# Differential attention heads: the probabilities become the stationary operand of the product with the values

## The reference

```python
s = jnp.einsum('bqhtd,bkhtd->bhtqk', qb, k).astype(jnp.float32) + bias[None, :, None]
pr = jax.nn.softmax(s, axis=-1)
attn = pr[:, :, 0] - lam * pr[:, :, 1]
...
o = rmsnorm(o, subln) * (1.0 - lam_init)
o = o.reshape(b, l, ATTN_V_DIM) * jax.nn.silu(z)
return o @ w_out
```

## Time and profile before

| | |
|---|---|
| median of 3 runs | 807.06 us (806.58 to 814.43) |
| the profiled execution | 812.39 us, of which the span of the trace is 810.4 us |
| PE matmul busy | 765.7 us, 94% of the span |
| DVE, ACT, POOL busy | 506.4, 402.6, 451.3 us |

### The profile page before, as it was taken

How to read it: one execution, slowest core, us unless ns; L and a number is a source line. 1 busy time by engine, 2 the same in 40 slices (tenths; PEclk the granted TensorE clock), 3 DMA queues, 4 the chain that set the end, 5 groups by cost and what they waited for, 6 DMA issues and landing times.

```text
span 810.4 us, 11587 instructions
## 1 busy us (share of the span) xinstructions
PE 765.7 (94%) x3856; PEld 616.9 (76%) x3856; DVE 506.4 (62%) x880; ACT 402.6 (50%) x806; POOL 451.3 (56%) x258
## 2 busy tenths in 40 slices
PE   4999999999999999998999999899999999998788
PEld 3677888888878787887878887667777777776576
DVE  4674957585858677785921131676867768677732
ACT  6446483829273655657332253355555454654410
POOL 5348595848484857665754427563653745536101
PEclk9999999999999999999999999999999999999999
DMA  9265464553626364543523214322313222220002
GB/s 255 78 196 127 159 151 162 124 189 95 190 82 160 125 155 154 155 158 104 210 78 107 82 52 143 112 74 66 88 53 101 76 78 74 67 85 27 0 1 104
DMA packets 100196, 91.10 MB, mean 112 GB/s; under 512 B 5456, under 2 KB 87728, under 8 KB 97080
## 3 DMA queue, kind: packets, MB, share of 16 engines
q1 hardware_dynamic: 95760, 66.99, 28.2%
q10 hardware_dynamic: 4264, 23.50, 9.3%
q0 software_dynamic: 128, 0.05, 0.0%
HBM read 88.13 MB, written 2.39 MB: 112 GB/s over the span
## 4 chain that ended last, share of the span: by engine, by line
PE 54%; DVE 20%; issue 11%; ACT 7%; POOL 7%; DMA 1%; DVEq 1%; ACTq 0%; SPq 0%; POOLq 0%
PE bank L1351 45%; DVE c_acc L996 6%; POOL w_lo L486 3%; POOL stat L477 2%; ACT ex L836 2%; PE bank L1454 2%; DVE sbias L1218 2%; PE bank L1428 1%; PE bank L1440 1%; DVE tmp L1038 1%; DVE ex L1229 1%; ACT qkvz L901 1%; ACT w_hi L621 1%; DVE stat L1222 1%; PE bank L1402 1%
## 5 line engine op out<-in xcount | busy, mean ns | idle before, releaser
L486 POOL TENSOR_TENSOR w_lo<-w_raw,w_hi 128x1024 fp32r<-128x1024 f32 x104 | 257.4, 2477 | 224.1 <-ACT w_hi L621 224.0
L1351 PE MATMUL bank<-hn_hi,w_hi 128*128 128x512 f32 (+1 forms) x392 | 157.9, 403 | 8.0 <-DVE BT L1011 5.0
L1351 PE MATMUL bank<-hn_hi,w_lo 128*128 128x512 f32 (+1 forms) x392 | 153.8, 392 | 0.0
L1351 PE MATMUL bank<-hn_lo,w_hi 128*128 128x512 f32 (+1 forms) x392 | 153.5, 392 | 0.0
L621 ACT CAST w_hi<-w_raw 128x1024 fp32r<-128x1024 f32 x104 | 108.7, 1047 | 71.5 <-PE bank L1351 68.5
L1351 PE MATMUL bank<-w_hi,hn_hi 128*128 128x512 f32 x320 | 131.0, 409 | 4.8 <-DVE hn_lo L1102 2.5
L1351 PE MATMUL bank<-w_lo,hn_hi 128*128 128x512 f32 x320 | 125.9, 393 | 0.0
L1351 PE MATMUL bank<-w_hi,hn_lo 128*128 128x512 f32 x320 | 125.9, 393 | 0.0
L996 DVE SCALAR_TENSOR_TENSOR c_acc<-bank,par,c_acc 128x510 f32<-128x510 f32 (+1 forms) x128 | 95.9, 749 | 24.0 <-ACT c_acc L665 14.6
L836 ACT ACTIVATE ex<-sbias,stat 128x512 f32<-128x512 f32 x64 | 45.7, 716 | 120.5 <-DVE stat L1222 120.5
L1351 PEld LDWEIGHTS bank<-hn_hi,w_hi 128*128 128x128 f32 (+1 forms) x392 | 73.5, 188 | 26.7 <-issue 9.9
(11 more groups left out here) (191 smaller groups left out, 1237.0 us busy)
## 6 DMA issues: line engine op xcount, KB each, us to landing
w_raw<-in_ssd_w_in SPq DMA_DIRECT2D x48, 512.0 KB, 4.0
w_raw<-in_attn_w_in SPq DMA_DIRECT2D x64, 256.0 KB, 3.1
rows<-acs_rows ACTq DMA_DIRECT2D x14, 1024.0 KB, 5.9
edec<-exp_rows ACTq DMA_DIRECT2D x16, 512.0 KB, 6.2
w_raw<-in_ssd_w_out SPq DMA_DIRECT2D x16, 512.0 KB, 3.5
w_raw<-in_attn_w_out SPq DMA_DIRECT2D x16, 256.0 KB, 3.1
wbias<-bias_rows SPq DMA_DIRECT2D x8, 448.0 KB, 4.1
rows<-in_x SPq DMA_DIRECT2D x4, 512.0 KB, 5.2
```

The lines of the kernel that those rows point to most:

```text
L486: nc.gpsimd.tensor_tensor(w_lo[:, s, :], w_raw[:, s, :], f32(w_hi[:, s, :]), ALU.subtract)\
L1351: ins = T.matmul(dst, a[i], b[j], start=first and n == 0, stop=last and n == 2)
```

## The change

`values` computes `o` directly instead of its transpose. The stationary operand is now a 128 x 128 block of `aT_hi` or `aT_lo` (128 keys, 128 queries), the moving operand is the 128 x 128 chunk of `v_hi` or `v_lo`. For each of four blocks of queries the four chunks of keys are summed: 4 x 4 x 3 = 48 matmuls of 128 columns in place of 12 of 512. The copy of bank 7 (L851) and the first four transposes (L1590) with their two semaphores are gone; ACT squares bank 7 in stage 0, where the copy stood.

```diff
-        o_copied, o_back = sem("o_copied"), sem("o_back")
...
                     if has(3):
                         act.wait_ge(pv_done, it - 2)
                         after(act, og_done, it - 3)
-                        nc.scalar.copy(o_chan[:, :], bank[7][:, :]).then_inc(o_copied, 1)
+                        nc.scalar.activation(o_flat, bank[7][:, :], ACT.Square).then_inc(o_sqd, 1)
...
-                    if has(3):
-                        act.wait_ge(o_back, it - 2)
-                        nc.scalar.activation(o_chan[:, :], bank[7][:, :], ACT.Square).then_inc(o_sqd, 1)
...
-                for c in range(NC):
-                    ins = product(bank[7][:, :], (v_hi[:, par_, c, :], v_lo[:, par_, c, :]),
-                                  (aT_hi[:, c, :], aT_lo[:, c, :]), c == 0, c == NC - 1)
+                for q in range(NC):
+                    rows_ = slice(q * P, (q + 1) * P)
+                    for c in range(NC):
+                        ins = product(bank[7][:, rows_], (aT_hi[:, c, rows_], aT_lo[:, c, rows_]),
+                                      (v_hi[:, par_, c, :], v_lo[:, par_, c, :]), c == 0, c == NC - 1)
                 ins.then_inc(pv_done, 1)
...
-                if s == 1 and has(3):
-
-                    pe.wait_ge(o_copied, it - 2)
-                    for c in range(NC):
-                        ins = T.transpose(bank[7][:, c * P:(c + 1) * P], o_chan[:, c * P:(c + 1) * P], ident[:, :])
-                    ins.then_inc(o_back, 1)
```

More of the change, by code:

```diff
@@ L295, in build @@
                     (stage[96:112, 2 * P:2 * P + 2], ssd_d.rearrange("a (t c) -> (a t) c", c=2)))
-        o_chan = o_sq[:, :, :].rearrange("p c n -> p (c n)")
+        o_flat = o_sq[:, :, :].rearrange("p c n -> p (c n)")
         f_rows = bias_fill[:, 0:2 * L]
```

## The result

The kernel after takes 841.82 us (median of 4, 841.2 to 842.1), the kernel before 807.63 us (median of 4, 806.58 to 814.43): a ratio of 1.0404, with a 95% interval of 1.0346 to 1.0461. That is slower, and above the predicted range, which ended at 838. The profiled execution after took 841.67 us, with a span of 839.9.

The account below looks back on a forecast made before the run. PE was taken to bound the full pipeline, chains through DVE, ACT and POOL the drain. Terms 22.8 - 2.6 - 0.4 - 1.8 - 1.4 = +16.6 us on 807.06 gave 823.7 us, range 809 to 838.

Parts of the forecast that it names:

- the price of the pair: In the values, one load and one 128-column float32r matmul on PE were to cost 0.116 us.
- (a): In the values, a pair costs its columns alone, 0.057 us; kernel at 801 us, not slower; chance 0.11.
- (b): In the values, a short float32r matmul is as slow as a 512-column one, 0.227 us; kernel 866 us; chance 0.13.
- the end of head 7 and the clock of the end: Behind head 7's values: square starts 1.81 us earlier, one wait goes, clock holds for the last projection: -1.8 and -1.4 us.
- ACT's copy and its waits: On ACT, one 0.59 us pass a head goes and the square moves to stage 0; effect in the loop 0.
- PE's waits growing in the loop: Sign in the attention loop: would show the prediction wrong in kind, another engine having become the bound.
- The transposes that go: Four PE transposes a head removed: 0.44 us each for heads 0 to 4, 0.4 for head 5; together 2.6 us saved.
- Rival (c): During each head's values the clock falls to 0.50, losing 1.5 us eight times, 12 us; kernel 836 us; chance 0.08.
- The values term: On PE, 48 short matmuls a head take 5.57 us, 2.85 more than before; 22.8 us over eight heads.

Follow-up runs that it names:

- e5: The kernel before with each 512-column stream of its values cut into streams of 256 columns, 24 matmuls a head: 811.28 us, ratio 1.0004.
- e1: The changed kernel with ACT's square of bank 7 put back from stage 0 into stage 1: 831.89 us, ratio 1.0311.
- e2: The kernel before with each 512-column stream of its values cut into four of 128, copy and transposes kept: 836.29 us, ratio 1.0361.
- e4: The changed kernel with POOL's weight split in stage 2 made to wait until DVE has scaled q and k: 830.21 us, ratio 1.0287.
- e8: The changed kernel with one piece of output projection moved from stage 6 to 7 of iteration 8, ahead of head 6's values: 832.09 us.

## Why the prediction was wrong

**Right: the price of the pair.** It was the term said to decide, 0.116 us from L1454's plain float32. It measured 0.11 us (5.31 us for 48), +2.6 us a head instead of +2.85. The stream is not what it costs, as forecast: e5's double streams cost only 0.12 us. That the load is what it costs stays the likely reason. The bounds of 0.057 and 0.227 us, rivals (a) and (b), were both far off. So was the 81 ns that the Trainium skill gives for such a pair ("TensorE: Matmul & The Clock Gate", "Back-to-back issue gap"): this trace has 0.11 us. The 107 ns that the Trainium skill gives for the load, in the same page's section "LDWEIGHTS (loading the stationary operand)", is close to it.

**Right: the end of head 7 and the clock of the end.** From head 7's values to the last projection it was +0.9 us for +1.05, and behind that -1.4 for -1.4, with the one wait (1.56 us) and the first matmuls fast (0.50 us, then 0.40), as forecast.

**The step that failed first: "ACT's copy and its waits".** It took ACT to be off the path ("PE doesn't wait for it: 0"), counted that no wait is added, and looked at what stands behind the square in stage 0. It didn't look at what stands behind the square's old place in stage 1: the cast of `w_hi`, for which POOL waits, which starts POOL's split, which was held behind DVE's scaling by nothing but that cast's lateness. An instruction that left ACT put POOL's start 0.3 us earlier against DVE's (0.18 us behind it, now 0.16 ahead), and DVE's scaling ended 2.1 us later. Of these 2.1 us PE lost 1.2 a head: 37.16 us in after against 35.94 in e1. Up to iteration 8's first fill that is 6.3 us, where the prediction had 0. Both signs were in the trace of before: the margin of 0.23 us in the timeline above, and a scaling of 3.40 us at 536.85, in iteration 2, where POOL's split had started at 536.78: the other order and its price. The prediction said that PE's waits growing in the loop would mean that another engine had become the bound; they grew, by 1.5 us a head, though DVE was not the bound by its busy time (25.54 of 37.17 us) but by one late instruction. The Trainium skill has this as a rule: "SBUF — State Buffer", section "SBUF: two separate sides", says that a VectorE operation with two inputs in SBUF and a GpSimd operation that reads SBUF lock each other out for a whole instruction, the first to start winning. The trace agrees: DVE's scaling ended 1.07 us after POOL's split (612.57 against 611.50), about its own length of 1.23 us.

**The second: "The transposes that go".** They were "saved whole" for heads 0 to 4, 2.2 us, because "every one removed is" a us of the kernel. The trace of before had a wait of 0.6 us in every head of the loop, so PE was not the only bound there; work taken out ahead of that wait only lengthens it. e1 and e2, with and without the transposes, take 35.94 and 35.95 us a head, and from the beginning of the attention to iteration 8's first fill 242.6 and 242.7 us: 0.1 us saved for 2.2. So a head in the loop is 33.34 + 2.59 (the pairs) + 0 (the transposes) + 1.22 (the late scaling) = 37.15 us, and 37.16 were measured from one scaling to the next. The pair, priced 0.26 us a head too high, hid part of this in the sum: that was luck.

**Rival (c) was of the right kind, with the wrong place and size.** It let the narrow values themselves pull the clock down, eight times for 1.5 us, at 8% and 12 us. In this trace they never did so from full clock (1.00 in head 7's values and in the loop). But started at the low clock they stayed there, once, for all 48: 10.27 - 4.43 = +5.84 us for head 6 instead of +2.85. A further 2.4 us is what is left of the surplus up to head 7's values, where the clock was at 0.50 until 793.3. The values term, 2.85 us for each of eight heads, was too small there. The prediction had the row of the 0.50 clock behind the idle stretches of the end, and asked it only of the end.

**The base.** 5 us of the miss lie here. The sum was put on a median of executions at a higher clock (806.7 against 812.5 us), while all four of the kernel after stood at 0.982. No trace of a faster execution of before is kept, so which stretches it has at full clock is not shown. In all, 841.8 - 823.7 = 18.1 us: 12.9 from the traces and 4.9 from the base (34.2 - 29.3, by execution times), the rest rounding.

Of the 12.9, the runs show the parts roughly. From the beginning of the attention on, e1 is 9.1 us shorter than after (without the new collision), e4 8.4, and e8 4.7 (with its values at full clock). e1 and e8 together make 13.8, above 12.9, as each changes a little more than its one cause: in e1 the stretch at 0.50 around head 6's values is also shorter, 13.7 us (from 768.1) for 17.1 in after (from 776.3). By the medians it would be 10 or 11.6 and 9.7, too much for 12.9; there the clock ahead of the attention is in it.

## What to carry to other kernels

When an instruction leaves an engine's list, follow what stood behind it, on that engine and on those that wait for it, to the first place where two engines that disturb each other start close together: a margin of 0.2 us decided some 10 us here. Before you count work taken from the busiest engine as gained, look for a wait behind it on that engine: 0.6 us a head was enough to swallow 0.44. A product of 128-column streams cost its number of loads here, twice as many in streams of 256 columns as good as nothing; swapping the operands to save a transpose pays only if the streams stay about that wide. And a product of short streams is badly placed behind an idle stretch of PE: moving a piece of wide work between them gained about 5 us.

## What the hardware showed that was not expected

- A DVE operation of 1.23 us took 3.30 when a POOL operation of 2.39 us had started 0.16 us earlier, and the POOL operation took 3.30 us when DVE had been 0.18 us ahead. DVE's scaling of one tensor by columns (L1229) was caught as well: 1639 ns at most instead of 546. There DVE had started 0.06 us before POOL's split (608.69 against 608.75) and lost all the same; POOL's power (607.77 to 608.78) was still running.
- 48 matmuls of 128 columns, back to back for 10.27 us, didn't bring the clock back from 0.50; behind 512-wide ones it was back within 3.0 to 3.4 us in e8's moved piece and in before, but only after 5.9 us in another place of e8 (789.0 to 794.9). Started at 1.00, the same 48 kept it.
- A float32r pair of 128 columns takes 0.11 us, one of 256 columns 0.12, one of 512 columns 0.227.
